# The last projected tile three slots earlier, six loads behind the barrier, and the order of the closing products

## The reference

```
h   = rms_norm(x);  p = h @ w_in                  # 1032 tokens, 1024 -> 3600 columns
FoX: softmax attention, 8 heads of 64, with cumulative log-forget bias
     (decode tokens attend to 1024 cached rows each, in 8 pages of 128)
GDN: q|k|v = silu(causal conv4(.)); q, k L2-normalised; gated delta rule in chunks, 4 heads of 128
     o = rms_norm(o) * out_norm * silu(z)
x   = x + concat(FoX out, GDN out) @ w_out
x   = x + (silu(conv3(h2 @ W_gate)) * (h2 @ W_up)) @ w_down;   y = rms_norm(x)
```

## Time and profile before

| | |
|---|---|
| time, median of 3 runs | 1809.84 us (1804.15 to 1815.65) |
| profiled execution: its own time, its span | 1811.04 us, 1809.5 us |
| TensorE busy | 1663.9 us, 92% of the span |
| VectorE, ScalarE, GpSimd busy | 955.6, 687.6, 521.0 us |
| granted TensorE clock, mean | 0.951 of full speed |
| DMA | 156 MB, 86 GB/s in the mean |

### The profile page before, as it was taken

How to read it: one execution, slowest core, us unless ns; L and a number is a source line. 1 busy time by engine, 2 the same in 40 slices (tenths; PEclk the granted TensorE clock), 3 DMA queues, 4 the chain that set the end, 5 groups by cost and what they waited for, 6 DMA issues and landing times. The chain is left out here.

```text
span 1809.5 us, 30580 instructions
## 1 busy us (share of the span) xinstructions
PE 1663.9 (92%) x10991; PEld 1571.9 (87%) x10991; DVE 955.6 (53%) x1711; ACT 687.6 (38%) x1085; POOL 521.0 (29%) x301
## 2 busy tenths in 40 slices
PE   6998998998997658988969999999999999999998
PEld 6897787797795547978959999999999999999998
DVE  4537558658648754364255554444444444545344
ACT  5424634634534532243253332222222222445344
POOL 5113323333232106234112222222222223445441
PEclk9999998999997869989979999999999999999999
DMA  5344443344343282003024311111111111211122
GB/s 155 105 118 109 126 147 104 107 148 122 100 141 107 78 311 79 1 18 114 1 92 147 101 41 47 47 47 47 47 47 47 47 47 47 111 48 51 44 65 95
DMA packets 213892, 156.04 MB, mean 86 GB/s; under 512 B 23617, under 2 KB 202721, under 8 KB 212848
## 3 DMA queue, kind: packets, MB, share of 16 engines
q1 hardware_dynamic: 168204, 117.85, 21.4%
q10 hardware_dynamic: 45064, 36.68, 6.5%
q0 software_dynamic: 512, 0.07, 0.1%
HBM read 122.90 MB, written 31.83 MB: 86 GB/s over the span
## 5 line engine op out<-in xcount | busy, mean ns | idle before, releaser
L207 PE MATMUL ps<-x_hi,w_hi 128*128 128x344 f32 x1584 | 508.3, 321 | 1.1 <-issue 1.1
L208 PE MATMUL ps<-x_lo,w_hi 128*128 128x344 f32 x1584 | 505.6, 319 | 0.0
L209 PE MATMUL ps<-x_hi,w_lo 128*128 128x344 f32 x1584 | 505.6, 319 | 0.0
L207 PEld LDWEIGHTS ps<-x_hi,w_hi 128*128 128x128 f32 x1584 | 297.6, 188 | 3.0 <-issue 1.4
L209 PEld LDWEIGHTS ps<-x_hi,w_lo 128*128 128x128 f32 x1584 | 298.0, 188 | 0.0
L208 PEld LDWEIGHTS ps<-x_lo,w_hi 128*128 128x128 f32 x1584 | 297.3, 188 | 0.1
L207 PE MATMUL ps<-h_hi,wm_hi 128*128 128x344 f32 x672 | 227.1, 338 | 1.6 <-ACT sqr L1188 1.0
L208 PE MATMUL ps<-h_lo,wm_hi 128*128 128x344 f32 x672 | 217.6, 324 | 0.0
L209 PE MATMUL ps<-h_hi,wm_lo 128*128 128x344 f32 x672 | 217.0, 323 | 0.0
L2423 POOL TENSOR_TENSOR w_lo<-w_raw,w_hi 128x1024 fp32r<-128x1024 f32 x42 | 110.0, 2619 | 371.2 <-ACT w_hi L2591 371.2
L2770 DVE TENSOR_TENSOR x_lo<-ffn_act,x_hi 128x2064 fp32r<-128x2064 f32 x36 | 87.1, 2420 | 122.9 <-ACT x_hi L2646 122.8
(11 more groups left out here) (408 smaller groups left out, 2916.1 us busy)
## 6 DMA issues: line engine op xcount, KB each, us to landing
w_raw<-in_w_up SPq DMA_DIRECT2D x44, 512.0 KB, 4.0
k_past<-in_cache_k SPq DMA_DIRECT2D x256, 64.0 KB, 1.9
v_past<-in_cache_v SPq DMA_DIRECT2D x256, 64.0 KB, 2.0
wm_raw<-in_w_in ACTq DMA_DIRECT2D x28, 512.0 KB, 4.2
w_raw<-in_w_down SPq DMA_DIRECT2D x44, 256.0 KB, 2.7
gdn_scratch<-conv ACTq DMA_DIRECT2D x12, 528.0 KB, 3.3
xT<-x_scratch SPq DMA_DIRECT2D x1, 4128.0 KB, 13.4
x_scratch<-xT SPq DMA_DIRECT2D x8, 516.0 KB
```

The lines of the kernel that those rows point to most:

```text
L207: pe.matmul(out, w_hi, a_hi, start=first, stop=False)
L208: pe.matmul(out, w_hi, a_lo, start=False, stop=False)
L209: return pe.matmul(out, w_lo, a_hi, start=False, stop=last)
```

## The change

Three things are done. First, the last tile's pieces go to the places that the table gives all tiles: slot 3 "b", slot 4 "a" and slot 4 "b" of step 3; its Silu and store then stand in slot 5 as they do in the steps before. Second, `load_first_pair` keeps gate rows, keys and values only; queries, decode states and z of pair 0 are loaded by SP at the beginning of the GDN stage, ahead of the loads of pair 1. Third, in the closing products of GDN VectorE multiplies o first by norm weight and Silu of z, which waits for the square only and in pair 0 stands ahead of the decode inputs of pair 1, and then by the reciprocal root.

```
 def piece_places():
             n = 3 + 7 * j + k // NG
-            if n == NTILES - 1:
-                slot, pos = LATE_PLACE[k % NG]
             if n < NTILES:
...
 def load_first_pair():
                     sp.dma_start(first.qkv[h][:, 2], v.gdn_dram[h, 2]).then_inc(first.v_loaded[h], 16)
-                for h in range(PAIR):
-                    sp.dma_start(first.qkv[h][:, 0], v.gdn_dram[h, 0]).then_inc(first.q_loaded[h], 16)
-                    sp.dma_start(blocks(first.s_dec[h]), t["state_gdn"][0, :, h:h + 1].rearrange("b a k e -> k (b a) e")).then_inc(first.s_loaded[h], 16)
-                    sp.dma_start(first.z_silu[h], v.gdn_dram[h, 3][:, 0:TOK]).then_inc(first.z_loaded[h], 16)
...
                 if i == 5:
                     need(act, conv_done, j, 3)
                     act.activation(conv[:, 2], conv[:, 2], ACT.Silu).then_inc(conv_silu.sem, 1)
-                    if j < STEPS - 1:
-                        silu_z()
+                    z = ext[:, 1, TAPS - 1:TAPS - 1 + TOK]
+                    act.activation(z, z, ACT.Silu).then_inc(conv_silu.sem, 1)
                     square(j, 1)
-                    need(act, conv_silu, j, 1)
+                    need(act, conv_silu, j, 2)
                     store(j, 2, conv[:, 2])
-                    if j < STEPS - 1:
-                        store_z(j)
+                    store(j, 3, z)
...
             for j in range(STEPS + 1):
-                if j == STEPS:
-                    silu_z()
-                    store_z(j - 1)
                 prologue(j)
...
+            for s, h in heads(0):
+                load_rest(s, h)
             for s, h in heads(1):
                 load_first(s, h)
...
                 for s, h in heads(pair):
                     decode_states(pair, s, h)
+                for s, h in heads(pair):
+                    need(dve, z_loaded[h], 0, 16)
+                    need(dve, osq_ready[s], pair, 1)
+                    dve.scalar_tensor_tensor(out=oT[s], in0=oT[s], scalar=v.out_norm[:], in1=z_silu[h], op0=ALU.mult, op1=ALU.mult)
                 if pair == 0:
                     for s, h in heads(1):
                         decode_inputs(1, s, h)
+                dve.drain()
                 for s, h in heads(pair):
-                    need(dve, z_loaded[h], 0, 16)
                     need(dve, orstd_ready[s], pair, 1)
-                    dve.scalar_tensor_tensor(out=oT[s], in0=oT[s], scalar=v.out_norm[:], in1=o_rstd[pair][s], op0=ALU.mult, op1=ALU.mult)
-                for s, h in heads(pair):
-                    dve.drain()
-                    dve.tensor_tensor(oT[s], oT[s], z_silu[h], ALU.mult).then_inc(o_ready[s].sem, 1)
+                    dve.tensor_tensor(oT[s], oT[s], o_rstd[pair][s], ALU.mult).then_inc(o_ready[s].sem, 1)
```

More of the change, by code:

```diff
@@ L684 @@
                (4, "a"), (4, "b"), (5, "a"), (5, "b"), (5, "c"), (6, "a"), (6, "b"), (6, "c"), (7, "a"), (7, "b"), (7, "c"))
-LATE_PLACE = ((5, "b"), (6, "a"), (6, "c"))
 EARLY_PIECES = 9
@@ L1287, in prologue @@
                     store(j - 1, 1, conv[:, 1])
[L1289 to L1296, removed]
             def slot(j, i):
```

## The result

The changed kernel takes 1797.24 us (median of 10 runs, 1789.40 to 1807.38), the kernel before 1812.85 us (10 runs on the same chip, 1804.15 to 1817.20): ratio 0.9914, 95% interval 0.9891 to 0.9936, so 15.6 us less, between 12 and 20. The forecast was 12.4 us less, 1797.4 us; that this lies 0.2 us from the measured time is luck, since the kernel before came out 3.0 us above the 1809.84 that the forecast started from and the gain 3.2 us larger. The profiled execution took 1792.71 us with a span of 1791.1 us (before 1811.04 and 1809.5) at a mean granted clock of 0.957 (before 0.951).

A forecast was written before the change was run, and what follows sets the result against it. The attention's last head step was taken as a chain hopping between engines, none full, bound by waits. Terms -5.5 + 0.5 - 1.2 - 3.7 + 0 - 2.5 = -12.4 from 1809.84 gave 1797.4 us, range 1788 to 1807.

The forecast's parts named there:

- C: Stretch from VectorE's first GDN instruction to the first update of the inverse; moved queries forecast at 0, upper end +5 us.
- Part 1, the tile: Last head step of attention: moving the tile's pieces gives -5.5 us in slot 6, costs +0.5 in slots 3 and 4.
- A: Stretch from slot 5's score round to issue of the decode store; moved tile forecast -5.5 us there, saved table load -1.2.
- Part 2, the table load: Attention's closing work: z's Silu moved into slot 5 saves the Exp table load before the decode weights, -1.2 us.
- Part 3, the loads: End of attention: with six loads moved, the decode store lands in 2.1 us instead of 5.8, -3.7 us.
- B: Stretch from issue of the decode store to VectorE's first GDN instruction; faster store landing forecast at -3.7 us.
- 0 for the queries: Start of GDN: moved query loads have 2 to 4 us of room before their first product, so cost 0.
- Part 4, the products: End of GDN: two of pair 1's four products move into the wait for the reciprocal root, -2.5 us; pair 0, 0.
- D: Stretch from pair 1's last state sum to the first work behind the barrier; reordered products forecast at -2.5 us.
- The clock takes back what the holes give: Slots 5 and 6: emptier TensorE stays at 1.2 GHz, the tile move gives 0, -6.9 us stays, 1803 us; chance 0.20.
- The queries come late: Start of GDN: a query load lands behind a state load and holds the chain, +5, 1802 us; chance 0.08.
- Slower, the pieces at half rate: Slots 3 and 4: pieces take 7 us each at low clock, slot 6 gives nothing, +2.1, 1812 us; chance 0.05.

The follow-up runs named there:

- e4: The kernel before with only the last tile's pieces moved, its z activation and store left in the closing work: 1802.84 us, ratio 0.9940.
- e11: The changed kernel plus matmuls on constants in TensorE's pauses of slots 5 to 7, spread to hold the clock up: 1795.62 us, ratio 0.9919.
- e7: The changed kernel without the last tile, its weight load, split, matmuls and evacuations left out: 1795.25 us, ratio 0.9913.
- e1: The kernel before with only the last tile and its z activation moved, loads and products as before: 1802.32 us, ratio 0.9942.
- e2: The kernel before with only the six query, state and z loads moved behind the barrier: 1809.73 us, ratio 0.9987.
- e5: The changed kernel with the six moved loads put behind the second pair's 14 loads on SP's queue: 1811.60 us, ratio 1.0004.
- e3: The kernel before with only the order of the closing GDN products changed: 1808.66 us, ratio 0.9979.
- e6: The changed kernel with the last tile's third piece kept in slot 6 and z back in the closing work: 1801.31 us, ratio 0.9952.

## Why the prediction was right, and where its sizes were off

The time fell by 15.6 us (12 to 20) where 12.4 were forecast; no step failed in its mechanism. The gains of all four parts were sized too small, and C, which the sum put at nothing, took a part of the surplus back.

**Part 1, the tile: -5.5 taken for slot 6, -7.3 measured** (A of e4; the cost in slots 3 and 4 lies ahead of A), about the -7 that the prediction gave as VectorE's limit. In the two profiles the way from slot 5's scores to the second half of the last score round shrank by 3.4 us (16.10 to 12.73; taken -2.3, at best 3.4), and from there to the last copy by 4.0 (17.07 to 13.08; taken -3.2, at best 4.6). The prediction discounted both for the clock. The clock was low indeed, 0.50 and 0.71 in the windows above, but it had been low in part of these slots before too, and the work that it slows is mostly hidden behind VectorE: with the clock at 1.00 (e11) only 2.6 us more come out. There the two stretches shrank to 11.53 and 11.44 us, by 4.6 and 5.6, so the "at best" of 3.4 and 4.6 were no bounds; in the first, VectorE's own work up to the first half of the scores took 8.86 us instead of 9.94. The added cost in slots 3 and 4 was taken at 0.5; the shift between the two profiles goes from -3.60 at the copy of 553.08 to -2.98 at 601.35, so 0.6 here, and e7 can't tell it from 0.

**Part 2, the table load: -1.2 taken, 1.5 measured** (A of e4 less that of e1). The wait itself went from 1.52 to 0.30. Between 520 and 700 us ScalarE loads 8 tables instead of 10; only the one on the path counts. The Trainium skill, "ScalarE: Activation LUTs", section "What ACT_TABLE_LOAD costs", gives some 1283 ns for the load, which the row of 1.28 us shows, and some 1380 ns more for a drain, 2.66 us per switch; of that second part the 1.5 us here leave no more than a few tenths.

**Part 3, the loads: -3.7 taken, -4.4 measured** (B, 7.49 to 3.10; in e2 as well). With the earlier tile but the old loads it is 8.43 (e1); the store there follows the first load by 15.4 us, in the kernel before by 18.2. Beside part 1 the move is worth 5.3. The store's landing, taken at 2.1, was 1.4 us. "0 for the queries" held: no wait of TensorE for a DMA in the changed kernel, keys and queries meet 12.1 us into the stage (662.55 - 650.47), as before. e5 shows that the room was real and small, and that the order on SP's queue is its condition. The sum put the beginning of the GDN stage at 0; C is +2.2 in this profile and +1.8 in the mean, of which about half goes with the clock, and the rest is open.

**Part 4, the products: -2.5 taken, -3.5 measured** (D, mean of the profiles with old products 17.63, with new 14.11). The two fused products behind the root are gone, 2.50 us, as taken. The two that stay no longer read z and take 2.38 instead of 2.56, and the first starts 1.10 us after ScalarE's root at 915.57 instead of 1.52 after that at 931.48. From the root to the first work behind the barrier it is thus 6.04 us instead of 9.21, 3.2 less; the step from the last product to that work is 2.56 in both, and the other 0.3 lie ahead of the root. For pair 0 the 0 agrees with the profiles: VectorE waits 3.0 to 5.1 us for TensorE behind these products in all of them. From the first update to pair 1's last sum it is 220.6 to 222.2 us in eleven profiles with products of either form; e3 and e6, both with the new order, have 225.6, but were 2.8 us late already ahead of pair 0's products, for a reason that stays open.

**The rivals.** *The clock takes back what the holes give* was half right: it does take some, 2.6 us by e11, not the whole of part 1. *The queries come late* is refuted for the order that was made and right for the order of e5. *Slower, the pieces at half rate*: the first piece did start at a clock of 0.51 (570 to 573 us) and took 5.6 us; by 576 the clock was 1.00 and the other two took 4.0 each, as the sum had it. e7 shows no cost that could be the rest.

## What to carry over

Where no engine is full, read the idle time ahead of the instructions that close a chain, and move only the work that stands in just those waits: a piece of 4 us behind VectorE's wait was worth 3.4 to 4.6, and in a pause of TensorE's own it cost nothing that could be seen. A small store that a barrier waits for lands late while the DMA engines are full of bulk loads; count the loads ahead of it, and keep what is needed early in the next stage first in that stage's queue. Sum the parts by their own stretches in the profile, since the time of the whole run told the products alone from nothing only just, and the loads alone not at all.

## What the runs showed that was not expected

The landing of one 4 KB store on another engine's queue went from 5.8 us to 1.4 us with eight 0.5 MB loads ahead instead of fourteen, and the stretch B from 3.1 to 6.2 us with ten, about half of that by the two loads. The room is narrow: in e7 the same eight loads went out up to 1.1 us later (the last at 635.21 instead of 634.10), the store landed in 2.7 us, and B is 4.40. Nor must all the loads have drained: in the kernel before the store landed some 5.8 us behind 658.88, and the windows from 660 to 666 us still show a DMA share of 1.03 to 1.14. That agrees with the Trainium skill, "DMA: Bandwidth & Descriptors", section "Issuing engines are not separate DMA queues", by which transfers of all engines run on the same 16 DMA engines and interleave. And the clock recovered through e11's filler came to 2.6 us in the profile of a stage whose TensorE is idle for a quarter of the time: full clock there is worth far less than the share of the low clock suggests.
